# One weight matrix in twelve loaded in three transfers instead of one, in a two-layer mixture-of-experts trunk

## What is computed

```python
g_p, g_idx = top_k(softmax(xf @ wg + bg), 1)            # one of 4 groups
top_v, top_i = top_k(e_logits of that group, 2)         # two of its 8 experts
gate = g_p * softmax(top_v)
# for every expert e, over the tokens sent to it (xb):
a = silu(xb @ w1[e]) * (xb @ w3[e])                     # w1, w3: 1024 x 512
y = a @ w2[e]                                           # w2: 512 x 1024
# y times its gate is added to the token's row
```

## Time and profile before

| | us |
|---|---|
| median of 3 runs (lowest to highest) | 1167.88 (1163.39 to 1168.81) |
| the profiled execution, its own time | 1163.12 |
| its span, first to last instruction | 1161.3 |
| TensorE busy, of the span | 876.3 |
| VectorE busy / ScalarE busy | 351.3 / 216.5 |

### The profile page before, as it was taken

One profiled execution on the slowest core, in us unless ns is written; L12 is line 12 of the kernel. 1 busy time (PEld: TensorE's weight loads), 2 busy tenths in 40 slices (PEclk: granted clock), 3 DMA queues, 4 the chain that ended last, 5 costly groups with the idle time before them and its releaser, 6 DMA issues.

```text
span 1161.3 us, 19468 instructions
## 1 busy us (share of the span) xinstructions
PE 876.3 (75%) x7954; PEld 507.3 (44%) x7955; DVE 351.3 (30%) x816; ACT 216.5 (19%) x487; POOL 5.1 (0%) x15
## 2 busy tenths in 40 slices
PE   6878776766676667588999987878775677677765
PEld 4544333433343334344787554444443343334432
DVE  3523322312231222223156433322332222213323
ACT  3221211111111111111145212210211121102112
POOL 1000000000000000000000000000000000000000
PEclk9899889979998998899999989989998899879888
DMA  9979999999999999997403429999999999999992
GB/s 308 404 286 426 426 422 425 426 426 424 424 426 426 424 424 427 425 426 308 184 1 150 170 116 404 427 426 424 426 426 426 423 424 427 426 423 424 427 400 98
DMA packets 33196, 427.74 MB, mean 368 GB/s; under 512 B 4292, under 2 KB 5572, under 8 KB 7704
## 3 DMA queue, kind: packets, MB, share of 16 engines
q1 hardware_dynamic: 32600, 424.18, 86.7%
q0 software_dynamic: 448, 1.25, 0.5%
HBM read 424.37 MB, written 1.05 MB: 366 GB/s over the span
## 4 chain that ended last, share of the span: by engine, by line
PE 43%; DMA 39%; DVE 8%; issue 6%; ACT 2%; DVEq 0%; SPq 0%; ACTq 0%
DMA ring<-in_moe_w 39%; PE ps L423 15%; PE ps L459 6%; PE ps L594 5%; PE ps L474 3%; PE ps L390 3%; DVE work L1019 2%; PE ps L580 2%; PE ps L648 2%; DVE work L1027 1%; ACT work L724 1%; PE ps L375 1%; ACT work L714 1%; DVE work L1021 1%; DVE work L1023 1%
## 5 line engine op out<-in xcount | busy, mean ns | idle before, releaser
L423 PE MATMUL ps<-ring,work 128*32 128x256 f32 x4224 | 316.7, 453 | 195.9 <-DMA ring<-in_moe_w 120.7
L423 PEld LDWEIGHTS ps<-ring,work 128*32 128x32 f32 x4224 | 169.9, 129 | 334.3 <-issue 247.7
L1017 DVE TENSOR_SCALAR work<-work 128x128 f32<-128x128 f32 (+1 forms) x64 | 14.7, 229 | 507.2 <-ACT work L724 507.2
L459 PE MATMUL ps<-ring,work 128*32 128x256 f32 x2112 | 128.7, 385 | 33.1 <-DVE work L1027 32.4
L390 PE MATMUL ps<-work,h_sb 128*128 128x256 f32 x576 | 145.6, 396 | 5.2 <-ACT work L714 4.5
L1053 DVE COPY hT<-ps 32x512 f32<-32x512 f32 x128 | 87.4, 683 | 146.4 <-PE ps L459 145.5
L390 PEld LDWEIGHTS ps<-work,h_sb 128*128 128x128 f32 x576 | 104.8, 192 | 57.2 <-issue 38.6
L724 ACT ACTIVATE work<-ps 128x256 f32<-128x256 f32 x64 | 24.6, 384 | 516.0 <-PE ps L423 516.0
L459 PEld LDWEIGHTS ps<-ring,work 128*32 128x32 f32 x2112 | 62.8, 110 | 97.2 <-DVE work L1027 48.2
L732 ACT COPY hT<-ps 32x512 f32<-32x512 f32 x128 | 74.1, 579 | 139.5 <-PE ps L459 138.8
L474 PE MATMUL ps<-hT,work 128*128 128x512 f32 x136 | 62.6, 604 | 12.2 <-DVE hT L1053 12.2
(11 more groups left out here) (147 smaller groups left out, 423.2 us busy)
## 6 DMA issues: line engine op xcount, KB each, us to landing
ring<-in_moe_w SPq DMA_DIRECT2D x192, 2048.0 KB, 29.5
ring<-in_attn_wv SPq DMA_DIRECT2D x2, 2048.0 KB, 32.8
ring<-in_attn_wq SPq DMA_DIRECT2D x2, 2048.0 KB, 31.8
ring<-in_attn_wk SPq DMA_DIRECT2D x2, 2048.0 KB, 33.4
ring<-in_attn_wo SPq DMA_DIRECT2D x2, 2048.0 KB, 37.2
x_sb<-in_x SPq DMA_DIRECT2D x2, 512.0 KB, 6.6
work<-in_pool_w SPq DMA_DIRECT2D x1, 1024.0 KB, 13.3
out_x<-h_sb SPq DMA_DIRECT2D x2, 512.0 KB, 3.3
```

Source lines behind the costliest of these rows:

```text
L423: mm = pe.matmul(gu_ps[SB * j:SB * (j + 1), b, :, :], xg[:, u, kt, b, k, :], w[:, :, kt, P * j:P * (j + 1)], start=(kt == 0 and b == 0), s ...
L459: mm = pe.matmul(y_ps[SB * i:SB * (i + 1), b, :], actT[:, b, SB * j:SB * (j + 1)], w[:, j, 256 * i:256 * (i + 1)], start=(j == 0 and b == ...
```

## The change

The w1 matrix of every fourth expert is sent as a transfer of rows 0 to 111 and two transfers of 8 rows, 112 to 119 and 120 to 127. The 112 rows are 7 for each of 16 DMA engines; each transfer of 8 rows gives one row to each of eight engines, so these carry 9 rows of the matrix and the other eight carry 7. The two small transfers raise a semaphore of their own, `w1_rest`, by 32 together, and TensorE waits for it as well before it uses such a matrix. All other matrices are sent as before. It applies to 8 matrices a layer; none of them is among a layer's first 8 chunks. The second pass is not changed.

```diff
+        w1_rest = sem("w1_rest")
...
+        def uneven(e, j):
+
+            return j == 0 and e % E4 == E4 - 1
...
+            def load_uneven(slot, src, signal):
+
+
+                sp.dma_start(ring[0:112, slot, :], src[0:112, :]).then_inc(signal, 16)
+                for p in (112, 120):
+                    sp.dma_start(ring[p:p + 8, slot, :], src[p:p + 8, :]).then_inc(w1_rest, 16)
...
                     sp.wait_ge(used[j], it * BODY + (layer * NE + e + 1))
-                    load(c % RING, chunk_parts(layer, it * BODY + c // CPE, c % CPE), loaded[c % RING])
+                    e, j = divmod(c, CPE)
+                    send = load_uneven if uneven(e, j) else load
+                    send(c % RING, chunk_parts(layer, it * BODY + e, j), loaded[c % RING])
...
                             pe.wait_ge(loaded[c % RING], (it * (CPE * BODY // RING) + (u0 + c // RING + 1)) * 16)
+                            if uneven(k, j):
+                                pe.wait_ge(w1_rest, (it * GPB + (layer * NGRP + gg + 1)) * 32)
                             return c % RING
```

## The result

The changed kernel takes 1383.1 us (median of 4 runs, 1367.8 to 1386.5), the kernel before 1167.9 on the same chip: a ratio of 1.183, 95% interval [1.178, 1.189]. The forecast was 1158.5. The loss is 215 us, or 215/16 = 13.4 us for each split matrix.

The account below looks back on a forecast made before the run. It took the DMA engines to bound the streams, with eight lagging at their ends. Saving 4.9 us a layer, -9.9 in sum, with about 0.5 left for small costs, gave -9.4 from 1167.9: 1158.5 us, range 1153 to 1216.

Parts of the forecast that it names:

- What bounds the kernel: Both expert streams: DMA engines set the pace at 425 GB/s, busy share 1.01; anything off them must be large to matter.
- The lag of eight engines: Streams' ends: eight engines finish 11.6 to 12.6 us behind on average, the last 14 to 16; instruction fetches assumed the cause.
- rival 2: Streams' ends: the eight engines given 9 rows are the lagging ones, 4.9 us later a layer, 1177.8 us; chance 0.12.
- Price of a narrow transfer: Small transfers: each row costs 0.617 us from below; from above 4.8 us per split matrix on eight engines; lower end taken.
- n: Factor by which a row of the 8-row transfers exceeds 0.617 us if engines share an SBUF input; hidden below 2.
- Rival 1: 8-row transfers: neighbouring rows share SBUF inputs, a row takes n times 0.617 us; n = 4 gives 1207 us; chance 0.32.
- Rows moved: Split w1 matrices: engines carrying 7 rows save 8 x 0.617 = 4.9 us a layer; the others gain 4.9, inside their lead.
- rival 3: Nothing gained: the lag is elastic, small costs eat the gain or the seven-row part loses it; 1163 to 1172; chance 0.10.
- The upper end of 1216: Top of the 8 in 10 range, covering the priced part of slower narrow rows, +48 us; leaves out a heavier form.
- Small costs: Split's own costs: about 0.5 us allowed; SP's two extra issues, 0.67 us per split matrix, and TensorE's wait taken as hidden.

Follow-up runs that it names:

- e_ballast: Kernel before plus, after every fourth expert's w1 matrix, two transfers of 8 rows of 16 KB from HBM to a spare HBM tensor: 1174.0 us, ratio 1.007.
- e_columns: Changed kernel with the split made by columns, 128 rows of 14 KB and twice 128 rows of 1 KB, same semaphores and waits: 1168.5 us.
- e_only112: Changed kernel without the two transfers of 8 rows and the wait on w1_rest, leaving rows 112 to 127 old: 1314.7 us.
- e_ballast8: Kernel before plus the same two 8-row HBM-to-HBM transfers, with 4080 elements a row and gaps so they can't be cut into 16 pieces: 1186.3 us, ratio 1.016.

## Why the prediction was wrong

**What bounds the kernel.** Right, and it is why the loss came out in full: nothing hid it. TensorE's wait for matrices goes from 121 to 284 us.

**The lag of eight engines.** Its existence and size stand: `e_ballast` and `e_columns` end with the same tail at half rate (199 to 214 GB/s over 10 us). That they are the engines that the change relieves was an assumption, and it was wrong for two of the eight. With no other effect the change would have made the last engine 4.9 us later a layer, 1177.8: rival 2, with two of the eight in place of all. "Each of those saves 8 x 0.617 = 4.9 us a layer, the last one too" failed here for the last one. That instruction fetches make the lag was not tested by any run.

**Price of a narrow transfer.** This step failed too. The prediction took 0.617 us a row, its lower bound, "because the queue is fed six matrices deep and nothing there shows a latency". That answers only to latency. The runs show no latency but rows that are slow: 2.0 us for each of the 8-row transfers' rows, n = 3.2. Rival 1 had the mechanism and its place, with n = 4 where the idle core shows 3.2. At n = 3.2 its own sum is (2 x 3.2 - 1) x 0.617 x 8 = 26.7 us a layer, less 16 and 14: about +23 us in all. The kernel pays some 65 us for these rows (215 less the 150 of `e_only112`), and two of the engines had no lead to give.

**Rows moved.** This is the step that failed by most. The prediction entered the 112 rows at 7 x 0.617 us on each engine, a saving of 4.9 us a layer; with them alone the kernel lost 150 us, 75 a layer. A 112-row transfer is not seven eighths of a whole one. It costs 1.02 us a row on its own, 3.8 us more than a whole matrix inside a stream on an idle core, and 9.4 us more in the kernel. That, cut into sevens, its engines' rows no longer match the inputs of SBUF is my reading; the runs show the price and not this. The prediction brushed it in rival 3 as a cut that "loses what it saves". The upper end of 1216 didn't price it at all, so the time lies 167 us above it.

**From 6.7 to 13.4 us a matrix.** On an idle core an odd matrix costs 6.1 to 7.4 us, and 11.2 in one queue. In the kernel the first of each layer costs 7 and later ones up to 17. My reading is that the engines drift apart as a stream runs, and that engines that reach the odd matrix at different times slow each other twice, once in their own odd rows and once as owners of an input that another's odd rows need. That the price is back at 7 in layer 1 fits it. It is argued, not shown: no run here held engines apart, and the cause of the second half of the loss stays open.

**Small costs.** SP's two further issues, the second semaphore and the wait are bounded by `e_columns`, which has them all, at 4 us in one run. The prediction had 0.5.

No form tried here beats the kernel before.

## What to carry to other kernels

Rows of a transfer aren't interchangeable: before moving a few of them to balance engines, measure a queue of transfers of just that shape on an idle core, which takes one run and here shows 57 us for 41. A busy share of 1.0 with a falling rate meant slow rows here, not a lack of work or latency. And a tail tells how many engines lag but not which; a ballast of just the change's transfers tells whether those engines are among them before the change is built on it. Look in the trace whether a probe did what it was built for: a ballast was cut over all 16 engines, and transfers meant to hold engines back by 12 us took SP as long to issue as they took to run.

## What the runs showed of the hardware that I had not expected

- Sixty-four rows of 16 KB take as long as 128 (41.3 and 41.0 us for eight), and 96 take longer (56.0).
- Eight engines end a long stream behind the others, but not the eight that an 8-row transfer uses: two of those and six others (tail of 49 to 61 GB/s in `e_ballast8`).
- The price of a split matrix grows within a stream, from 7 to 17 us, and starts at 7 again in the next one.
- Eight adjacent rows of 16 KB from HBM to HBM were cut into 16 pieces of 8 KB and ran on all 16 engines; with gaps between the rows they ran on eight (512 and 256 packets of under 512 B more for 32 transfers).
- TensorE's granted clock was 0.845 of full speed in the mean after the change for 0.912 before, and 0.50 (1.2 for 2.4 GHz) in the windows from 150 to 160 us, where it did nothing. Its gate and up products went from 453 to 473 ns in the mean. In the streams the DMA engines' share stays at 1.00 to 1.01 all the same, so they didn't wait for it.
